# Input projection ahead of its norm: the root applied at the copy out of PSUM, sums behind the first tile, two weight slabs right behind x

## What is computed

```
h = rmsnorm(x, g[0])        # x * rsqrt(mean(x*x) + 1e-6) * gain
z = h @ w_in                # 2048 x 6016 weights: 47 tiles of 128 columns
qkv, sgu, rwkv = split(z)   # then attention, gating and an RWKV scan on z
```

## Time and profile before

| | us |
|---|---|
| median of 3 runs | 3180.11 (3180.01 to 3181.32) |
| the profiled execution | 3179.2 |
| its span in the trace | 3177.4 |
| TensorE busy | 3040.5, 96% of the span |
| VectorE busy | 1570.8, 49% |
| ScalarE busy | 1266.5, 40% |
| in the chain that ended last: TensorE | 87% |

### The profile page before, as it was taken

How to read it: one execution, slowest core, us unless ns; L and a number is a source line. 1 busy time by engine, 2 the same in 40 slices (tenths; PEclk the granted TensorE clock), 3 DMA queues, 4 the chain that set the end, 5 groups by cost and what they waited for, 6 DMA issues and landing times.

```text
span 3177.4 us, 51930 instructions
## 1 busy us (share of the span) xinstructions
PE 3040.5 (96%) x21496; PEld 2642.4 (83%) x21496; DVE 1570.8 (49%) x2402; ACT 1266.5 (40%) x1925; POOL 17.9 (1%) x34
## 2 busy tenths in 40 slices
PE   6999999899889999999998999999999999999997
PEld 6966666698779999999996888778878998889896
DVE  4444434544365556564445323554553474247744
ACT  4322112343445444443434223444542472245544
POOL 0000000000000000000000000000000000000000
PEclk9999999899989999999999999999999999999998
DMA  7577777544435555545553222222223443234442
GB/s 231 183 292 313 311 316 286 199 141 151 146 119 183 179 181 184 182 156 181 175 191 110 93 93 80 80 80 90 91 99 119 159 161 105 92 118 146 141 152 106
DMA packets 74279, 509.69 MB, mean 160 GB/s; under 512 B 8460, under 2 KB 8588, under 8 KB 20240
## 3 DMA queue, kind: packets, MB, share of 16 engines
q1 hardware_dynamic: 70416, 486.08, 42.9%
q0 software_dynamic: 3712, 21.40, 2.1%
HBM read 500.89 MB, written 6.55 MB: 160 GB/s over the span
## 4 chain that ended last, share of the span: by engine, by line
PE 87%; DVE 6%; ACT 3%; DMA 2%; issue 1%; SPq 0%; ACTq 0%; DVEq 0%
PE bank L685 39%; PE bank L1220 8%; PE bank L780 5%; PE bank L1251 5%; PE bank L1253 5%; PE bank L1252 5%; PE bank L797 2%; PE bank L730 1%; PE bank L731 1%; PE bank L732 1%; PE bank L936 1%; PE bank L876 1%; DMA high_f<-in_w_in 1%; DVE ring_f32r L1972 1%; PE bank L1289 1%
## 5 line engine op out<-in xcount | busy, mean ns | idle before, releaser
L1972 DVE TENSOR_TENSOR ring_f32r<-ring_f,high_f32r 128x1024 fp32r<-128x1024 f32 (+1 forms) x692 | 780.7, 1159 | 794.8 <-ACT high_f32r L1405 793.5
L1405 ACT CAST high_f32r<-ring_f 128x1024 fp32r<-128x1024 f32 (+1 forms) x692 | 655.8, 997 | 881.4 <-PE bank L685 535.9
L685 PE MATMUL bank<-y_f32r,high_f32r 128*128 128x256 f32 (+1 forms) x2784 | 852.6, 306 | 23.3 <-DVE ring_f32r L1972 10.9
L685 PE MATMUL bank<-h_f32r,high_f32r 128*128 128x256 f32 (+1 forms) x2208 | 685.9, 311 | 4.3 <-DVE y_f32r L1972 3.4
L685 PE MATMUL bank<-y_f32r,ring_f32r 128*128 128x256 f32 (+1 forms) x2208 | 673.3, 305 | 0.0
L685 PEld LDWEIGHTS bank<-y_f32r,high_f32r 128*128 128x128 f32 x2784 | 535.3, 192 | 47.1 <-issue 22.2
L685 PEld LDWEIGHTS bank<-h_f32r,high_f32r 128*128 128x128 f32 x2208 | 422.9, 192 | 26.7 <-issue 4.5
L685 PEld LDWEIGHTS bank<-y_f32r,ring_f32r 128*128 128x128 f32 x2208 | 424.2, 192 | 17.2
L1251 PE MATMUL bank<-h_f32r,high_f32r 128*128 128x512 f32 x512 | 209.3, 409 | 0.0
L780 PE MATMUL bank<-h_f,high_f 128*128 128x256 f32 x768 | 196.4, 394 | 9.5 <-DMA high_f<-in_w_in 9.5
L1253 PE MATMUL bank<-h_f32r,ring_f32r 128*128 128x512 f32 x512 | 200.1, 391 | 0.0
(11 more groups left out here) (413 smaller groups left out, 4925.1 us busy)
## 6 DMA issues: line engine op xcount, KB each, us to landing
ring_f<-in_w_in SPq DMA_DIRECT2D x135, 1024.0 KB, 4.9
ring_f<-in_w_mod SPq DMA_DIRECT2D x96, 1024.0 KB, 8.9
ring_f<-in_w_up SPq DMA_DIRECT2D x88, 1024.0 KB, 4.9
ring_f<-in_w_out SPq DMA_DIRECT2D x56, 1024.0 KB, 4.9
ring_f<-in_w_down SPq DMA_DIRECT2D x64, 704.0 KB, 4.0
high_f<-in_w_in SPq DMA_DIRECT2D x24, 1024.0 KB, 5.0
ring_f<-in_w_kv SPq DMA_DIRECT2D x8, 1024.0 KB, 5.0
ring_f<-in_w_q SPq DMA_DIRECT2D x4, 1024.0 KB, 4.9
```

Of the source, the lines that this page charges most:

```text
L685: last = mm(bk[(t0 + j) % banks][:, 0:width], w[:, c], x[:, k], start=(k == 0 and w is hi and x is rhs.hi), stop=(k == KC - 1 and w is lo))
L1405: act.copy(w_hi[p % 2][:, half], slot[s % SLOTS][:, half]).then_inc(w_high, 1)
L1972: return v.tensor_tensor(out, in0, in1, op)
```

## The change

The vector of small weights is loaded ahead of x. The first two slabs are asked for without a wait for x. VectorE multiplies x by the gain alone, one quarter at a time, and splits it. TensorE does tile 0 at once, then the 16 partial sums of the squares (now kept in H[1]), then tile 1 with the closing sum inside, tiles 2 to 4, the two small matmuls, and the other 18 tiles. ScalarE no longer copies tiles out: VectorE does, multiplying by the reciprocal root. The copy of the line and what follows it move behind tile 6's copy. H[0] gets its root at tiles 8 to 11, for the later plain tiles. VectorE's steps from L2077 on stay behind all of this.

```
@@ -342,6 +342,7 @@
         sgu_t = Z[:, 44:48]
         sgu_g = tiles(arena[:, H1_AT + 10 * T:H1_AT + 14 * T], 512)
         out1_sq = Z[:, 28:44]
+        in1_sq = H[1]
         rx = Area(X1_AT, KC * T)
         krw = rx.take(P + 7 * CH + T)
         head_ones, mask2 = krw[:, 0:P], krw[:, P:2 * P]
@@ -433,10 +434,10 @@
         @block.sync
         def _(sp):
             sp.dma_start(kbase, d["k_base"]).then_inc(S("base_loaded"), 16)
+            sp.dma_start(vecs, d["vecs"]).then_inc(loaded, 16)
             for q in range(4):
                 c = slice(q * KC * T // 4, (q + 1) * KC * T // 4)
                 sp.dma_start(x_all[:, c], d["xT"][:, c]).then_inc(S(f"x_loaded{q}"), 16)
-            sp.dma_start(vecs, d["vecs"]).then_inc(loaded, 16)
             WEIGHTS = {"in1": "w_in", "kva": "w_kv", "out1": "w_out", "kvb": "w_kv", "q": "w_q", "wo": "w_o",
                        "up": "w_up", "down": "w_down", "in20": "w_in2", "out20": "w_out2", "out20_x": "w_out2",
                        "out20_ctx": "w_out2", "in21": "w_in2",
@@ -459,8 +460,9 @@
                 sp.dma_start(to, src[k, :, :] if isinstance(k, int) else
                              src[bass.ds(k, 1), :, :].rearrange("a p n -> p (a n)")).then_inc(done, 16)
 
-            sp.wait_ge(S("x_loaded3"), 16)
             for k in range(23):
+                if k == 2:
+                    sp.wait_ge(S("x_loaded3"), 16)
                 if k >= SLOTS:
                     sp.wait_ge(gemm_done, k - SLOTS + 1)
                 sp.dma_start(slot[k % SLOTS], d["w_in"][k, :, :]).then_inc(w_in_slot[k % SLOTS], 16)
@@ -719,7 +721,8 @@
                 r = RHS[rhs]
                 n, p, sl = TILE0[name] + t, SPLIT0[name] + t, SLAB0[name] + t
                 pe.wait_ge(w_split, p + 1)
-                pe.wait_ge(gemm_free, n - 1)
+                if n > 1:
+                    pe.wait_ge(gemm_free, n - 1)
                 hi, lo = w_hi[p % 2], w_lo[sl % SLOTS]
                 for k in range(KC):
                     if k in between:
@@ -755,8 +758,16 @@
                         2: {0: lambda: (squares_summed(s, 0), squares_summed(s, 1)), 3: lambda: squares_summed(s, 2),
                             7: lambda: squares_summed(s, 3), 13: lambda: finish_sum(T, 6, s * T)}}
 
+            tile3("in1", 0, "in1", {}, RHS0["in1"])
             pe.wait_ge(S("base_loaded"), 16)
-            colsum4(H[0], T, 7)
+            all_sums[0] += 1
+            sums[0] += 4
+            for k in range(KC):
+                if k % 4 == 0:
+                    pe.wait_ge(sq_ready, k // 4 + 1)
+                part_sum(in1_sq, T, 7, k)
+            tile3("in1", 1, "in1", {3: lambda: finish_sum(T, 7)})
+            gemm3("in1", 2, 3, rhs="in1")
             pe.wait_ge(loaded, 16)
 
             pe.wait_ge(S("mix_loaded"), 16)
@@ -765,7 +776,7 @@
 
             pe.wait_ge(S("lam_line_made"), 1)
             mm(bk[3][:, 0:4], ones, lam[:, 0:4], start=True, stop=True).then_inc(S("line_lam_mm"), 1)
-            gemm3("in1", 0, 23)
+            gemm3("in1", 5, 18, rhs="in1")
 
 
 
@@ -1463,13 +1474,11 @@
                         act.wait_ge(S(f"x_loaded{q}"), 16)
                     f(H[0][:, c], X[0][:, c], ACT.Square).then_inc(sq_ready, 1)
 
-            squares_of_x(0)
-            root()
+            rhs_highs("in1")
             high("in1", 0)
-            rhs_highs("in1")
+            for q in range(4):
+                f(in1_sq[:, 4 * q:4 * q + 4], X[0][:, 4 * q:4 * q + 4], ACT.Square).then_inc(sq_ready, 1)
             high("in1", 1)
-            act.wait_ge(S("line_lam_mm"), 2)
-            f(lam[:, 4:8], bk[3][:, 0:4], ACT.Exp).then_inc(S("lam_exp"), 1)
 
             def lora_inputs():
                 act.wait_ge(S("lora_mixed"), 1)
@@ -1478,8 +1487,16 @@
                 f(lora_g[1], Z[:, 46, :], ACT.Sigmoid)
                 act.copy(lora[1][64:P, :], Z[64:P, 44, :]).then_inc(S("rw_lora"), 1)
 
-            evac("in1", lambda t: at(Z, t + 3) if isinstance(t, int) and t >= 21 else at(Z, t + 26), n=23,
-                 between={22: lora_inputs})
+            for t in range(21):
+                act.wait_ge(gemm_done, t + 1)
+                high("in1", t + 2)
+                if t == 0:
+                    root()
+                if t == 5:
+                    act.wait_ge(S("line_lam_mm"), 2)
+                    f(lam[:, 4:8], bk[3][:, 0:4], ACT.Exp).then_inc(S("lam_exp"), 1)
+            lora_inputs()
+            act.wait_ge(gemm_free, 23)
 
 
             def beside1(m, i, z):
@@ -2049,30 +2066,45 @@
             def gains(n):
                 return vec("g")[:, n * KC:(n + 1) * KC]
 
-            dve.wait_ge(S("base_loaded"), 16)
             dve.wait_ge(loaded, 16)
             tt(lam[:, 0:4], vec("lamq"), vec("lamk")).then_inc(S("lam_line_made"), 1)
-            rstd(D, RMS1_EPS, parts=True)
+            for q in range(4):
+                dve.wait_ge(S(f"x_loaded{q}"), 16)
+                for k in range(4 * q, 4 * q + 4):
+                    last = ts(H[0][:, k, :], X[0][:, k, :], gains(0)[:, k:k + 1])
+                last.then_inc(rhs_made, 1)
+                if q:
+                    rhs_low("in1", q - 1)
+            rhs_low("in1", 3)
             low("in1", 0)
-            rhs_made_and_split("in1", norm_quarter(H[0], X[0], gains(0)))
             low("in1", 1)
-            dve.wait_ge(S("lam_line_made"), 1)
-            dve.wait_ge(S("line_lam_mm"), 1)
-            v.tensor_copy(g_line[0:A_HEADS, :], bk[2][0:A_HEADS, 0:384]).then_inc(S("lam_line_made"), 1)
-
-            dve.wait_ge(S("lam_exp"), 1)
-            step(tt(lam[:, 8:10], lam[:, 4:6], lam[:, 6:8], ALU.subtract))
-            for layer in range(2):
-                init = 0.8 - 0.6 * math.exp(-0.3 * layer)
-                step(ts(lam[:, 10 + layer:11 + layer], lam[:, 8 + layer:9 + layer], -1.0, -init))
-                sub = vec("subln")[:, layer:layer + 1]
-                step(ts(sub, sub, 1.0 - init))
-            dve.wait_ge(S("mix_loaded"), 16)
-            dve.wait_ge(S("sgu_loaded"), 9 * 16)
-            step(tt(sgu_w, sgu_w, spread(kmix[:, 384:512], 8)))
-            dve.sem_inc(S("sgu_masked"), 1)
-
-            lows("in1", 2, 21)
+            gather(T, 7)
+            low("in1", 2, halves=(0,))
+            rstd(D, RMS1_EPS)
+            for t in range(23):
+                dve.wait_ge(gemm_done, t + 1)
+                tt(Z[:, t + 26 if t < 21 else t + 3, :], bk[t % 2][:, 0:T], stat[:, 0:T]).then_inc(gemm_free, 1)
+                if t < 21:
+                    low("in1", t + 2, halves=(1,) if t == 0 else (0, 1))
+                if t == 6:
+                    dve.wait_ge(S("lam_line_made"), 1)
+                    dve.wait_ge(S("line_lam_mm"), 1)
+                    v.tensor_copy(g_line[0:A_HEADS, :], bk[2][0:A_HEADS, 0:384]).then_inc(S("lam_line_made"), 1)
+
+                    dve.wait_ge(S("lam_exp"), 1)
+                    step(tt(lam[:, 8:10], lam[:, 4:6], lam[:, 6:8], ALU.subtract))
+                    for layer in range(2):
+                        init = 0.8 - 0.6 * math.exp(-0.3 * layer)
+                        step(ts(lam[:, 10 + layer:11 + layer], lam[:, 8 + layer:9 + layer], -1.0, -init))
+                        sub = vec("subln")[:, layer:layer + 1]
+                        step(ts(sub, sub, 1.0 - init))
+                    dve.wait_ge(S("mix_loaded"), 16)
+                    dve.wait_ge(S("sgu_loaded"), 9 * 16)
+                    step(tt(sgu_w, sgu_w, spread(kmix[:, 384:512], 8)))
+                    dve.sem_inc(S("sgu_masked"), 1)
+                if 8 <= t < 12:
+                    c = slice(4 * t - 32, 4 * t - 28)
+                    step(tt(H[0][:, c], H[0][:, c], spread(stat[:, 0:T], 4)))
 
             dve.wait_ge(gemm_free, TILE0["in1"] + 21)
             dve.wait_ge(S("line_stored"), 16)
```

## The result

The changed kernel takes 3185.84 us (median of 20 executions, 3183.74 to 3190.27), the kernel before in the same rounds 3179.41 (3176.32 to 3183.39). The ratio is 1.0021, interval 1.0015 to 1.0027: slower by 6.4 us, or 0.2% (4.8 to 8.6 us by the interval). The profiled execution took 3184.6 us with a span of 3182.8, which is 5.4 us above the span before.

A forecast was written before the change was run, and what follows sets the result against it. TensorE, busy 49.77 of 50 us after the projection, bounds the kernel, so the first 180 us decide. Terms -2.9 + 1.0 + 0 + 7.8 = +5.9 on 3179.2 give 3185.1, with 0.9 for the median 3186.0 us; range 3178 to 3191.5.

The forecast's parts named there:

- Opening, first matmul 19.3: Start of the projection: first matmul at 19.3 us instead of 24.0; whole opening -2.9 us, ends -1.0 and -4.0.
- Tile 0 8.5 us, sums 1.9, chain of the root ending as tile 1 does: First two tiles: tile 0 ends at 27.8, tile 1 at 35.9, VectorE's chain at 35.8; tile 2 starts 2.9 us earlier.
- Two small matmuls +1.0: L763 and L767, now between tiles 4 and 5 with nothing hiding them: +1.0 us, ends +0.9 and +2.0.
- Steady tiles 0: Later projection tiles: VectorE's added copies, steps and products are covered by TensorE's 5.75 us per tile, so 0.
- The skew 0, with +4.0 if the time counts from the skew's issue: Stall behind the skew transfer: stays 8.0 us counted from the slab's issue, 12.0 from the skew's; ends -1.7 and +4.0.
- Rival A: Delay counts from the skew's own issue, slab 11 meets all of it: stall 12.0, total +9.9, 3190.0 us; chance 0.2.
- The seam +7.8: Projection's end: TensorE waits for lora inputs, made behind VectorE's last copy, and loses clock; +7.8 us, ends +7.2 and +8.6.
- Rival B: Skew and slab 11 share evenly, no stall and no cold restart: -9.3, total -3.4, 3176.7 us; chance 0.1.
- C: At the projection's end the lora steps are not exposed and cost 0: total -1.9, 3178.2 us; chance 0.1.
- D: Opening gives nothing (x behind slabs, or chain behind the first sum 3 us late): total +8.8, 3188.9 us; chance 0.07.
- The range: Whole kernel: 3178 to 3191.5 us stated; the terms' ends were given as +2.4 to +12 us.
- The sign "TensorE's waits after 180 us differ from before": After the projection: the prediction called itself wrong if TensorE's waits there differed from before; no size given.

The follow-up runs named there:

- the last skew experiment: Changed kernel with the skew transfer waiting for the end of tile 7, issued 0.3 us behind slab 11's issue; one execution of 3187.26 us.

## Why the prediction came out right

The forecast was 3186.0 us with a loss of 5.9, and 3185.84 with 6.4 was measured; it called this within 0.2% and it lies on that edge (1.0021), as the text had it "near its upper edge". That the absolute times agree to 0.2 us is luck: single executions spread over 3183.7 to 3190.3, and the kernel before had a median of 3180.11 in the first three and of 3179.41 in all twenty. That its steps hold one by one is not. By its steps:

- **Opening, first matmul 19.3.** It came at 18.54. x landed at 7.08 and not 7.4, and VectorE's chain took 11.4 us from the first product to the split slab, 11.9 forecast. The row is the earliest of the seven kernels with these loads (7.08 to 7.97, first matmul 18.54 to 19.46); by the second tile's end they lie between 34.94 and 35.83, and the three traces of the kernel before and its variants between 38.44 and 39.02. The opening's gain at this place is so 2.6 to 4.1 us, 3.4 on average.
- **Tile 0 8.5 us, sums 1.9, chain of the root ending as tile 1 does.** 8.5 us (18.54 to 27.04), 1.86, and the chain ended 0.3 us ahead. Tile 2 started 3.5 us earlier, -2.9 forecast. The difference is the first matmul's 0.8, of which x's landing is 0.3 and VectorE's shorter chain 0.5, less 0.2 on the way to the end of tile 1.
- **Two small matmuls +1.0.** 0.74 and 0.32 us, 1.06.
- **Steady tiles 0.** Casts stand 5.76 us apart as before.
- **The skew 0, with +4.0 if the time counts from the skew's issue.** The stall was 8.13 against 8.04. Slab 11 was asked for at 71.1 and there at 92.8, 21.7 us, exactly slab 5's time, although the skew had a lead of 1.6 us and not of 5.4; from the skew's issue it was 23.3 against 27.1. With the last skew experiment the times from the late slab's own issue are 21.7, 21.7 and 22.3, those from the skew's issue 27.1, 23.3 and 27.4. Rival A is gone. The Trainium skill, "DMA: Bandwidth & Descriptors", section "Queues, rings and completion order", says that each DMA engine takes turns between queues and changes only at the end of a packet. The runs agree with a count from the slab's own issue; that it comes from packets is not shown, since nothing here shows their turns.
- **The seam +7.8.** L791 moved from E + 7.3 to E + 15.0, +7.7. The wait was 7.13 (7.1 forecast), the two short waits of 1.2 were covered, and clock cost 1.6 (7.87 us from L907 to L791, 6.27 with the silence filled), 1.9 forecast. Here too the profiled execution stands at one end: the same stretch behind the same 7.13 us took 9.13 us with the skew in parts and 8.94 with the skew behind slab 11, which is 2.9 and 2.7 of clock. The same delay put into the kernel before gave 1.0022, and taking it out of the changed one gave 0.9997 and 0.9996.
- **Rival B** (even sharing, no stall) did not happen: the stall was 8.13, **C** (the lora steps not exposed) is refuted by those same runs, **D** (no gain in the opening) by the trace.
- **The range.** The upper ends of the terms give +13.6 (-1.0 + 2.0 + 4.0 + 8.6) and not +12. The range that was stated did not use it.
- **The sign "TensorE's waits after 180 us differ from before"** did show, in a small way (98.1 us against 96.2), without moving the total. It was too strict as it was put.

The sum of what the profile shows, -3.5, +1.06, +0.1, some 0.2 of further small differences, and +7.7, is +5.6; the span says +5.4. So the size was right and not only the direction. The opening was 0.6 us better than forecast; 0.4 us of small terms, most of them put at nothing, took over half of that back, and the seam was equal to 0.1.

## What to carry to other kernels

When work moves from one engine's queue to another's, look at what stands behind it in the new queue: here two copies that nobody waited for soon stood ahead of steps for which TensorE did wait, and their place cost twice what the whole opening won (7.7 us against 3.5). A long transfer can hold the slabs of a prefetch ring for longer than the ring's lead: here 21.7 us against 13.7. Cut into four parts, issued 7.6 to 11.5 us apart, it made TensorE wait for nothing. Count the clock with every silence of several microseconds: here 1.3 to 2.9 us on top of 7 to 8.

## What the runs showed of the hardware that was not expected

- The delay of a slab behind the skew hardly depends on when the skew began: 21.7, 21.7 and 22.3 us with the skew 5.4 us ahead, 1.6 us ahead and 5.1 us ahead of the slab, against 4.8 to 5.1 us for the slabs of the changed kernel asked for from 46.9 to 65.3. The next two slabs in the changed kernel, asked for while the skew's 36.1 us ran, took 23.3 and 23.4 us. A slab asked for 0.7 us ahead of the skew's issue landed in 5.0 us. In the changed kernel with the skew in parts the slabs took 5.8 to 11.6 us.
- Half clock behind a silence of 7.1 us lasted to the end of L910 in the changed kernel (178.1) and longer in the run with the skew in parts, where the 24 matmuls of the modulation product took 3.86 us and not 2.78. There the granted clock is 0.50 until 170.0. The same silence so costs 1.6 us in one execution and 2.9 in another. Behind the skew's stall it is alike: the matmuls keep half pace until 99.2 in the changed kernel (stall of 8.13 us) and until 102.7 in the run in which ScalarE copies tiles 21 and 22 (8.27 us).
- The landing of x varied from 7.1 to 8.0 us between executions with the same loads, as much as several terms of the sum.
- In the opening the clock column reads 1.00 while the matmuls run at half the later pace (28 in 5.9 us), in both kernels.
